# Attention's scores and weighed values in alternating halves of TensorE's array

## The reference

```python
logits = jnp.einsum('bnqhgd,bnkhd->bnhgqk', q, k) * (HEAD_DIM ** -0.5)
logits = jnp.where(valid, logits + bias, -jnp.inf)
m = jnp.maximum(jnp.max(logits, axis=-1, keepdims=True), sink)
p = jnp.exp(logits - m)
denom = jnp.sum(p, axis=-1, keepdims=True) + jnp.exp(sink - m)
o = jnp.einsum('bnhgqk,bnkhd->bnqhgd', p / denom, v)
```

## Time and profile before

| | |
|---|---|
| median of 3 runs | 1976.27 us |
| lowest, highest | 1974.50, 1977.24 us |
| span of the profiled execution | 1976.8 us |
| busy: PE / DVE / ACT / POOL | 1502.9 / 1252.3 / 672.8 / 625.4 us |
| bytes moved by DMA | 645.41 MB |
| mean granted clock of PE | 0.820 of 2.4 GHz |

### The profile page before, as it was taken

One profiled execution on the slowest core, in us unless ns is written; L12 is line 12 of the kernel. 1 busy time (PEld: TensorE's weight loads), 2 busy tenths in 40 slices (PEclk: granted clock), 3 DMA queues, 4 the chain that ended last, 5 costly groups with the idle time before them and its releaser, 6 DMA issues.

```text
span 1976.8 us, 23093 instructions
## 1 busy us (share of the span) xinstructions
PE 1502.9 (76%) x7810; PEld 712.3 (36%) x7810; DVE 1252.3 (63%) x2812; ACT 672.8 (34%) x1742; POOL 625.4 (32%) x594
## 2 busy tenths in 40 slices
PE   6999899999878878768887666666666676566665
PEld 2787678898753435423333111111111111000000
DVE  2067643666565664876766667766676678677654
ACT  2135443411233443643533223342232234223222
POOL 1000000000024333344444444454444445444441
PEclk9999999899989999869988765775767776766566
DMA  9543243200559999999999999999999999999996
GB/s 315 147 141 107 89 140 130 75 22 22 224 202 404 418 416 412 419 380 419 420 420 419 421 421 417 422 403 421 421 419 418 419 407 363 422 421 421 421 422 262
DMA packets 100182, 645.41 MB, mean 326 GB/s; under 512 B 11561, under 2 KB 11617, under 8 KB 32053
## 3 DMA queue, kind: packets, MB, share of 16 engines
q0 software_dynamic: 77536, 558.01, 69.1%
q1 hardware_dynamic: 22528, 85.93, 12.1%
HBM read 638.75 MB, written 6.18 MB: 326 GB/s over the span
## 4 chain that ended last, share of the span: by engine, by line
DMA 38%; PE 37%; DVE 11%; ACT 6%; issue 6%; POOL 1%; another core or an unknown queue 1%; DVEq 0%; ACTq 0%; SPq 0%; POOLq 0%
DMA arena<-in_euv,consts 36%; PE abank L813 21%; PE fsum L1364 6%; PE dbank L813 4%; DVE arena L2014 4%; PE dbank L1364 2%; ACT consts L794 1%; PE abank L1280 1%; DMA arena<-in_wstream 1%; ACT arena L457 1%; ACT small L787 1%; POOL arena L440 1%; DVE arena L1610 1%; DVE arena L1746 1%
## 5 line engine op out<-in xcount | busy, mean ns | idle before, releaser
L2014 DVE CUSTOM_DVE_ANT_0 arena<-arena 128x1024 f32<-128x1024 f32 x520 | 633.9, 1224 | 420.2 <-DMA arena<-in_euv,consts 411.0
L440 POOL DMA_INDIRECT arena<-in_euv,consts x520 | 589.8, 1134 | 777.4 <-PE fsum L1364 540.4
L1364 PE MATMUL fsum<-arena,consts 128*32 128x512 f32 x1536 | 505.5, 837 | 307.0 <-ACT consts L794 303.9
L813 PE MATMUL abank<-arena 128*128 128x256 f32 (+4 forms) x2400 | 541.8, 384 | 11.3 <-DVE arena L1610 3.9
L813 PEld LDWEIGHTS abank<-arena 128*128 128x128 f32 (+1 forms) x2400 | 404.7, 193 | 163.1 <-issue 63.1
L787 ACT ACTIVATE small<-small 128x1 f32<-128x1 f32 x520 | 104.8, 202 | 719.5 <-DVE small L2014 712.9
L1364 PEld LDWEIGHTS fsum<-arena,consts 128*32 128x32 f32 x1536 | 60.9, 124 | 686.5 <-ACT consts L794 666.0
L1364 PE MATMUL dbank<-arena,consts 128*32 128x512 f32 x512 | 157.2, 808 | 98.7 <-ACT consts L794 98.2
L457 ACT ACTIVATE arena<-abank 128x512 f32<-128x512 f32 (+5 forms) x228 | 111.3, 488 | 316.3 <-PE abank L813 298.2
L794 ACT ACTIVATE consts<-arena,small 128x32 f32<-128x32 f32 (+1 forms) x520 | 166.9, 321 | 17.8 <-ACT small L787 0.7
L813 PE MATMUL dbank<-arena 128*128 128x128 f32 (+6 forms) x784 | 117.1, 313 | 0.7 <-ACTq L620 0.7
(11 more groups left out here) (289 smaller groups left out, 1149.8 us busy)
## 6 DMA issues: line engine op xcount, KB each, us to landing
arena<-in_wstream SPq DMA_DIRECT2D x132, 512.0 KB, 4.2
arena<-in_euv,consts POOLq DMA_INDIRECT x520
arena<-in_wout SPq DMA_DIRECT2D x8, 1024.0 KB, 10.4
arena<-mod SPq DMA_DIRECT2D x7, 512.0 KB, 12.5
arena<-in_x POOLq DMA_DIRECT2D x1, 2048.0 KB, 15.0
arena<-in_sdel POOLq DMA_DIRECT2D x1, 2048.0 KB, 8.4
out_deltas<-arena POOLq DMA_DIRECT2D x1, 2048.0 KB, 6.8
out_yp<-arena SPq DMA_DIRECT2D x4, 512.0 KB
```

The lines of the kernel that those rows point to most:

```text
L440: pool.indirect_dma_start(ring[n % SLOTS], None, I["euv"], bass.IndirectOffsetOnAxis(cur[:, u % 2, c:c + 1], 0)).then_inc(ring_in[n % SLOT ...
L813: return pe.matmul(out, lhsT, rhs, start=first, stop=last)
L1364: last = pe.matmul(out[e][to:to + 32, :], S[:, n // NQ % 2, n % NQ, :], v, start=h == 0 and kk == 0, stop=h == PH - 1 and kk == 3, skip_gr ...
L2014: TTR(uh, uh, rep[j] if t < NT else h2sb, 1.0, 0.0, ALU.mult, ALU.add, dot[:, n // NQ % 2, n % NQ:n % NQ + 1]).then_inc(s.dots_done, 1)
```

## The change

The matmuls are the same ones with the same shapes; their order differs, and the bank that a score lands in. In the scores, the two heads of a pair of banks are issued in the order (h, h+4, h+1, h+5), the first of each couple into one bank, the second into the other, and both banks are claimed ahead. In the values, the matmuls are sorted so that a part of head h is followed by the same part of head h+4. In the decode rows' scores the loop over the two key/value heads becomes the inner one. DVE's reader takes the banks in the new order of heads.

```diff
             def attention_scores(blk):
 
                 lo = 0 if blk else P
-                for i in range(HQ // 2):
-                    b = dring.to_fill()
+                for a in range(HG // 2):
+                    banks = [dring.to_fill(), dring.to_fill()]
                     for e in range(2):
-                        h = 2 * i + e
-                        g, half = h % HG, slice(64 * (h // HG), 64 * (h // HG) + 64)
-                        last = mm(b[:, e * 256 + lo:e * 256 + 256], qT[half, g, blk * P:(blk + 1) * P],
-                                  kT[half, (blk - 1) * P + lo:(blk + 1) * P])
-                    last.then_inc(s.dring_full, 1)
+                        for kv in range(2):
+                            half = slice(64 * kv, 64 * kv + 64)
+                            last = mm(banks[kv][:, e * 256 + lo:e * 256 + 256], qT[half, 2 * a + e, blk * P:(blk + 1) * P],
+                                      kT[half, (blk - 1) * P + lo:(blk + 1) * P])
+                            if e == 1:
+                                last.then_inc(s.dring_full, 1)
...
             def values_weighed(blk):
                 pe.wait_ge(s.probT_ready, blk + 1)
                 b = aring.to_fill()
-                for i, (h, c) in enumerate(heads_and_halves(blk)):
+                parts = heads_and_halves(blk)
+                for i in sorted(range(len(parts)), key=lambda i: (parts[i][0] % HG, parts[i][1], parts[i][0] // HG)):
+                    h, c = parts[i]
                     half = 64 * (h // HG)
...
             pe.wait_ge(s.kTs_ready, 1)
-            for kv in range(2):
-                b = dring.to_fill()
-                half = slice(64 * kv, 64 * kv + 64)
-                for q in range(NB):
-                    last = mm(b[:, q * HG:(q + 1) * HG], probT[half, q, :], qT[half, :, SEQ + q])
-                last.then_inc(s.dring_full, 1)
+            banks = [dring.to_fill(), dring.to_fill()]
+            for q in range(NB):
+                for kv in range(2):
+                    half = slice(64 * kv, 64 * kv + 64)
+                    last = mm(banks[kv][:, q * HG:(q + 1) * HG], probT[half, q, :], qT[half, :, SEQ + q])
+                    if q == NB - 1:
+                        last.then_inc(s.dring_full, 1)
...
                 for i in range(HQ // 2):
                     b = dring.to_read()
-                    step(STT(prob[:, 2 * i:2 * i + 2, lo:256], three(b[:, :], 256)[:, :, lo:256], HD ** -0.5,
-                             bias[:, 2 * i:2 * i + 2, lo:256], ALU.mult, ALU.add), s.dring_free)
+                    here = slice(2 * (i // 2) + HG * (i % 2), 2 * (i // 2) + HG * (i % 2) + 2)
+                    step(STT(prob[:, here, lo:256], three(b[:, :], 256)[:, :, lo:256], HD ** -0.5,
+                             bias[:, here, lo:256], ALU.mult, ALU.add), s.dring_free)
```

## The result

The changed kernel takes 1964.55 us (median of 6 runs, 1961.94 to 1971.30) against 1976.31 us of the kernel before beside it (6 runs, 1971.68 to 1977.80): a ratio of 0.9947, 95% interval 0.9930 to 0.9963. 1964.3 us had been forecast.

What follows compares the result with a forecast made beforehand. PE was taken to bound attention among the projections, with gains passing through the DMA-bound expert retrieval; 9.7 us from the groups plus 2.8 from the clock gave 12.5 off 1976.8, so 1964.3 us, range 1961.5 to 1970.0.

Steps and rivals of the forecast that it cites:

- What bounds it: PE bounds attention among the projections; its 4.6 us wait moves along, and gains before the first expert fetch pass through.
- The groups: Scores, values and decode scores overlap fully at one half's pitch: 2.9 + 0.55 + 4.6 + 1.7, taken as 9.7 us.
- The lower bounds: Groups' saving if scores overlap no deeper than a crossing, 4.6 us; if the partner trails half a step, 9.2 us.
- Waits and covers: Claiming two score banks at once and DVE's new order of heads cost nothing; if a cover went, below 1 us.
- The clock: Behind the shorter decode scores PE's clock holds at full instead of falling to half, giving back 2.8 us.
- rival A: The clock falls all the same around the decode scores; only 9.7 us won, 1967.1 us; chance 0.24.
- The sum: Groups' 9.7 plus the clock's 2.8 gives 12.5 us off the span of 1976.8, so 1964.3 us; chance 0.57.
- B: Column halves can't be kept fed when matmuls change sides; values save nothing, 7.9 us won, 1968.9 us; chance 0.04.
- C: PE's wait at 222.8 swallows 6.6 us won before it; 5.9 us left, 1970.9 us; chance 0.06.
- D: A half's second record holds up the other half; only the old crossings' overlap remains, 1976.8 us; chance 0.04.
- E: Every change of halves costs a first step and nothing overlaps; 10.4 us slower, 1987.2 us; chance 0.02.

Runs made afterwards that it cites:

- e4: The whole change once more, on chip 3, against the kernel before: 1958.07 against 1967.09 us, ratio 0.9950 (0.9932 to 0.9969).
- e5: The whole change, but halves take turns after every two matmuls instead of every one: scores 2.10, values 2.02, decode scores 1.97 us a group; no total given.
- e9: The whole change repeated on chip 12 against the kernel before: 1957.61 against 1965.91 us, ratio 0.9945 (0.9924 to 0.9966).
- e8: The kernel before, unchanged, profiled again on chip 3: scores 2.96, values 3.33, decode scores 3.87 us a group; no ratio given.

## Why the prediction was right, and where it wasn't

- **What bounds it.** Right. PE's order from 105 us on sets the time, its wait of 4.6 us moves with it (4.59 before, 4.61 after), and what is won before the first fetch moves the later stage forward: fetch and decode scores moved by 12.03 and 8.95 us, DMA share unchanged. That the way behind the first fetch keeps its length is shown to within the 3 us by which it varies. Up to T, 6.6 us had been expected (0.55 + 2.9 + 0.5 + 2.7) and 6.64 were measured.
- **The groups.** Right in each term: scores 2.00 of 2.00 us and 1.16 of 1.15; values 1.97 of 1.97 and 1.10 of 1.09; decode scores 1.95 of 1.99. In sum 9.71 of 9.7. Some 0.35 us of the decode scores' 1.72 are the clock's by the estimate above, which the prediction counted with the group; the sum of both terms stays. The lower bounds, no overlap beyond a crossing (4.6) and a partner half a step behind (9.2), weren't needed. What made these terms safe was that the trace of before held both the pitch within one half and a group that alternated already. Two readings of these rows were loose and did no harm. The 0.32 us of the first step is that of the matmul records; the loads are 0.11 and then 0.22 apart. And the seven loads in 0.64 us and nine in 0.38 count those that were under way when the stretch began: five and six start in it, against three and 3.5 of one half alone.
- **Waits and covers.** Right: no wait of DVE for scores appears, and PE claims its two banks without waiting.
- **The clock.** The step that failed. That the fall cost 2.8 us behind the decode scores was sound (2.88 measured). That the clock holds behind 2 us of thin matmuls was taken from one stretch with six of them, and of seven profiles with a group of 1.95 to 1.97 us only three bear it out, after not among them. There the fall was half as long and gave back 1.20 us, so the truth lay between the forecast and rival A. Neither had a value between all and nothing, and it was there that a third case was missing. The prediction asked how long the thin stretch lasts; the table of the clock's falls above says that it should also have asked when the group comes.
- **The sum.** 9.7 + 1.2 + 0.1 = 11.0 us of the change's own, 1.5 less than forecast. The profile's remaining 2.7 are the earlier S (0.96) and the shorter retrieval (1.74). So the right total for the change is nearer 1976.8 - 11.05 = 1965.8 than the 1963.0 of that span; the timed ratios of three comparisons, 0.9947, 0.9950 and 0.9945, are 9.8 to 10.8 us, each with an interval of some 3 to 4 us on either side, and agree with it.
- **Rivals.** B, C, D and E are refuted by lengths, not by the total: the values' 1.97 us, the constant wait, the groups' gain and the group lengths of e4 and e5, in which changes of halves cost almost nothing. For B that means also: by the Trainium skill, TensorE: Matmul & The Clock Gate, Part 3, "The mechanism", loads overlap only where row groups differ; the trace doesn't agree, since 32 records of column halves, all in one row group, took 1.97 us instead of 3.33.

**What stays open.** Why the clock fell in some profiles behind the same 1.95 us and not in others: the moment at which the group comes is argued, not tested. And whether the two row halves may write to the same bank at once without loss: both kernels give each half its own, and it wasn't tried. (The column halves of the values do share one bank, at 1.97 us.)

## What to carry to other kernels

Matmuls that use half of the array's rows or columns should be issued so that no more than some four records (two float32 matmuls) of one half follow each other; here strict turns made 3.33 us into 1.97 and 2.96 into 2.00, and turns of two matmuls 2.02 and 2.10. Measure the pitch within one half and at one crossing in the trace you have: it gave every group's new length to 0.04 us. And before counting idle time as slack, ask who ends it: here the engine that waits was also, two steps earlier, the one that set the end of its wait.

## What the runs showed of the hardware that I hadn't expected

- The gain of two halves isn't a factor of two: 1.69 for values (3.33 / 1.97) and 1.48 for scores (2.96 / 2.00), since the old order already overlapped at its crossing and each group has its first step and run-out.
- The fall of the clock came in two sizes, 6.8 and 3.4 us, at a price of 2.88 and 1.68 us in the same stretch of work, and it fell 99.0 us after its last return, wherever the decode scores lay. A repeated kernel may show it at different later places: X to G took 221.97 us in e9 and 218.36 in e4, the same program, and e9's clock was at half at 432 and at 490 us, where e4's was not.
- The retrieval starts at different speeds in different profiles of one program: POOL's first fetch to its eighth, which waits for a buffer of the ring, takes 22.6 us (before) and 24.0 us (after) in the first two profiles, and 18.1 us in e8 as in e4 on chip 3 and in e9 on chip 12. That the chip is the reason is likely, not shown. The eighth fetch of after, and that of e4 (start, length, what, in brackets the idle time before and what ended it):

```profile
554.46 1.04 POOL L440 DMA_INDIRECT arena<-in_euv,consts  x1 [0.29 <-POOL consts L431]
...
578.47 1.48 POOL L440 DMA_INDIRECT arena<-in_euv,consts  x1 [15.45 <-PE fsum L1368]
```

```profile
552.17 1.03 POOL L440 DMA_INDIRECT arena<-in_euv,consts  x1 [0.29 <-POOL consts L431]
...
570.29 1.49 POOL L440 DMA_INDIRECT arena<-in_euv,consts  x1 [9.56 <-PE fsum L1368]
```
